# A two-layer block on one core: the first mixer's row shifts move from GpSimd's DMA queue to ACT's, with the gate job first and the parameter loads in three parts

## The reference

```
mod = silu(c) @ ada_w + ada_b                      # six rows of 1024: shifts, scales, gates
h = rms_norm(x, norm1_g) * (1 + sc1) + sh1
z = h @ w_in                                       # 2072 columns for fox, 1824 for rwkv
# fox (8 heads of 64)
k = a_k * shift_prev(k) + (1 - a_k) * k            # a_k = sigmoid of a gate column; v likewise
q, k = rms_norm(q), rms_norm(k)
cum = cumsum(log_sigmoid(f_logit + forget_b))      # over the tokens
o = softmax(causal(q k / 8 + cum_q - cum_k)) v
# rwkv (8 heads of 64)
zr = zr + mu * (shift_prev(zr) - zr)               # over all 1824 columns: r, k, v, low-rank parts
w, a, g = low-rank products of tanh / sigmoid parts of zr
o = wkv7_scan(r, w, k, v, -kk, kk * a)
x = x + g1 * (concat(fox, rwkv) @ w_out)
```

## Time and profile before

| | us |
|---|---|
| median of three timed runs (lowest, highest) | 1726.18 (1723.91, 1727.97) |
| the profiled execution | 1728.36 |
| its span in the profile | 1726.4 |
| TensorE busy, share of the span | 1420.5, 82% |
| DVE, ACT, POOL busy | 677.0, 392.9, 130.2 |

### The profile page before, as it was taken

How to read it: one execution, slowest core, us unless ns; L and a number is a source line. 1 busy time by engine, 2 the same in 40 slices (tenths; PEclk the granted TensorE clock), 3 DMA queues, 4 the chain that set the end, 5 groups by cost and what they waited for, 6 DMA issues and landing times.

```text
span 1726.4 us, 17781 instructions
## 1 busy us (share of the span) xinstructions
PE 1420.5 (82%) x6756; PEld 892.2 (52%) x6756; DVE 677.0 (39%) x1203; ACT 392.9 (23%) x620; POOL 130.2 (8%) x51
## 2 busy tenths in 40 slices
PE   5865845667897899999999999589968667599996
PEld 1432414666754444444444444366546436399974
DVE  2006227544446322222222222453365522457652
ACT  0101114132101121222222122234220111344442
POOL 0012224284000000000000000000000000000000
PEclk8887965787987899999999999689859987699998
DMA  9732101153127099999999997644411121145551
GB/s 326 215 122 74 47 17 72 57 186 126 49 90 309 36 402 422 412 420 409 416 421 420 415 413 302 229 146 146 75 48 50 49 98 49 49 149 171 170 172 72
DMA packets 105390, 338.76 MB, mean 196 GB/s; under 512 B 20465, under 2 KB 46484, under 8 KB 76537
## 3 DMA queue, kind: packets, MB, share of 16 engines
q1 hardware_dynamic: 84162, 319.08, 48.2%
q10 hardware_dynamic: 9528, 15.46, 3.3%
q0 software_dynamic: 11648, 3.50, 0.9%
HBM read 332.94 MB, written 1.05 MB: 193 GB/s over the span
## 4 chain that ended last, share of the span: by engine, by line
PE 68%; DVE 15%; DMA 5%; another core or an unknown queue 3%; ACT 3%; issue 2%; ACTq 2%; POOL 1%; DVEq 0%; SPq 0%; POOLq 0%
PE bank L1621 13%; PE bank L1637 7%; PE bank L1221 6%; PE bank L1240 6%; PE bank L1242 5%; PE bank L1241 5%; DMA z_prev<-z_rw 3%; PE bank L1584 2%; PE bank L1442 2%; DMA ring<-in_w_in 2%; PE bank L1585 2%; PE bank L1602 2%; PE bank L1604 2%; PE bank L1252 2%
## 5 line engine op out<-in xcount | busy, mean ns | idle before, releaser
L1221 PE MATMUL bank<-ring,xT 128*128 128x512 f32 (+3 forms) x480 | 203.0, 579 | 47.5 <-ACT z_rw L801 20.6
L1221 PEld LDWEIGHTS bank<-ring,xT 128*128 128x128 f32 x480 | 94.6, 213 | 146.3 <-issue 119.6
L1637 PE MATMUL bank<-dn,tmp 128*64 128x512 f32 x528 | 120.6, 598 | 0.0
L1240 PE MATMUL bank<-mod,w_high 128*128 128x256 f32 x352 | 101.6, 289 | 11.5 <-DVE xT L2948 5.3
L2574 DVE TENSOR_TENSOR xT<-bank,mod 128x512 fp32r<-128x512 f32 x66 | 45.7, 692 | 157.9 <-ACT mod L998 150.6
L1241 PE MATMUL bank<-xT,w_high 128*128 128x256 f32 x352 | 99.9, 284 | 0.0
L2567 DVE SCALAR_TENSOR_TENSOR tmp<-silu_c,rc,bank 128x256 f32<-128x256 f32 x33 | 22.6, 686 | 196.8 <-ACT silu_c L985 191.4
L1242 PE MATMUL bank<-mod,ring 128*128 128x256 f32 x352 | 99.5, 283 | 0.0
L2937 DVE TENSOR_TENSOR ring<-ring,w_high 128x1024 fp32r<-128x1024 f32 x66 | 77.6, 1220 | 26.2 <-ACT w_high L1163 24.6
L1252 PE MATMUL bank<-c_ident,xn 128*128 128x128 f32 x120 | 28.0, 412 | 63.7 <-DVEq L2637 25.4
L2015 POOL TENSOR_TENSOR ring<-ring 128x2048 f32<-128x2048 f32 x16 | 72.9, 4557 | 77.5 <-ACT ring L893 76.9
(11 more groups left out here) (581 smaller groups left out, 2563.1 us busy)
## 6 DMA issues: line engine op xcount, KB each, us to landing
dn<-in_exp_w_down SPq DMA_DIRECT2D x66, 1024.0 KB, 10.6
ring<-in_exp_w_gate SPq DMA_DIRECT2D x34, 1024.0 KB, 9.0
ring<-in_exp_w_up SPq DMA_DIRECT2D x34, 1024.0 KB, 10.8
gu_odd<-in_exp_w_gate SPq DMA_DIRECT2D x32, 1024.0 KB, 10.1
gu_odd<-in_exp_w_up SPq DMA_DIRECT2D x32, 1024.0 KB, 12.2
ring<-in_w_ffn_in SPq DMA_DIRECT2D x22, 1024.0 KB, 5.1
ring<-in_ada_w SPq DMA_DIRECT2D x16, 1024.0 KB, 4.9
ring<-in_w_in SPq DMA_DIRECT2D x7, 2048.0 KB, 27.8
```

The lines of the kernel that those rows point to most:

```text
L1221: mm = pe.matmul(bank[lin_bank(o)][:, 0:n], lhs(k, t), ring[:, j % RING, k * n:(k + 1) * n], start=(k == 0), stop=(k == kt - 1 and not bias))
L1240: pe.matmul(out, w[0], x[0], start=start, stop=False, skip_group_check=True)
L1637: mm = pe.matmul(bank[6 + h][CHUNKS[c], :], act_eT[:, 0, k, CHUNKS[c]], dn[:, 2 * parity + c, lo:lo + BANK], start=(k == 0), stop=(k == D_ ...
```

## The change

- The gate columns become the first input job; their copies, the gate sigmoid and the forget chain move to the head of ACT's list, and PE's small sum stands behind the key job.
- ACT issues the three fox gains and `mu` first, the constants and low-rank matrices after the key copies, and the seven rwkv rows and norm2_g after the value copies and the shift of keys and values.
- All five shifts are issued by ACT, each when the copies of its group are done; for KR and VR also after the lerp that used the same buffer two groups before. POOL keeps the row clears and the lerps.
- The receptance copies stand ahead of the two roots.
- Semaphores follow: `forget_loaded` counts four loads, `mu_loaded` is new, `par_loaded` counts the constants too, `zr_shifted` is one per buffer.

```diff
-        IN_JOBS = [(512, 512), (1024, 512), (2048, 24), (0, 512),
+        IN_JOBS = [(2048, 24), (512, 512), (1024, 512), (0, 512),
                    (FOX_COLS + 1536, 288), (FOX_COLS, 512), (FOX_COLS + 512, 512), (FOX_COLS + 1024, 512), (1536, 512)]
...
+            def shift_rows(dst, src, landed):
+
+                act.dma_start(dst[1:P, :, :], src[0:P - 1, :, :]).then_inc(landed, 16)
+                act.dma_start(dst[0:1, 1, :], src[P - 1:P, 0, :]).then_inc(landed, 16)
+
+            def shift_group(i, j):
+
+                lo, width = IN_JOBS[j]
+                act.wait_ge(lin_evac, after(j, 1))
+                if i >= 2:
+                    act.wait_ge(lerp_done, i - 1)
+                shift_rows(z_prev[:, i % 2, :, 0:width], z_rw[:, :, lo - FOX_COLS:lo - FOX_COLS + width],
+                           zr_shifted[i % 2])
...
+            for t in range(T):
+                in_copy(J_K, t)
             for name in CONST_1:
-                act.dma_start(cst[name][:, :], consts[name]).then_inc(const1_loaded, 16)
...
+                act.dma_start(cst[name][:, :], consts[name]).then_inc(par_loaded, 16)
...
+            for t in range(T):
+                in_copy(J_V, t)
+            act.wait_ge(lin_evac, after(J_V, 1))
+            shift_rows(kv_prev, z_fox[:, :, 512:1536], kv_shifted)
+            for i, name in enumerate(("rw_w0", "rw_a0", "rw_k_k", "rw_k_a", "rw_r_k", "rw_lnx_g", "rw_lnx_b")):
+                act.dma_start(rwp[:, i, :], bcast(A[name])).then_inc(par_loaded, 16)
             act.dma_start(gain[:, 1, :], bcast(A["norm2_g"])).then_inc(gain_loaded[1], 16)
...
+            for t in range(T):
+                in_copy(J_Q, t)
+            for i, j in enumerate((J_LORA, J_R)):
                 for t in range(T):
                     in_copy(j, t)
+                shift_group(i, j)
             rstd(fs[:, 6, 0:16], fs[:, 5, 0:16])
             rstd(fs[:, 8, 0:16], fs[:, 7, 0:16])
-            for t in range(T):
-                in_copy(J_R, t)
             act.wait_ge(lerp_done, 1)
...
             for t in range(T):
                 in_copy(J_KR, t)
+            shift_group(2, J_KR)
...
                     in_copy(J_VR, h - 1)
+                    if h == 2:
+                        shift_group(3, J_VR)
...
+            dense(J_FG, first_lhs)
+            dense(J_K, xTk)
             pe.wait_ge(logf_ready, 1)
...
-            for j in (J_LORA, J_R, J_KR):
+            for j in (J_V, J_Q, J_LORA, J_R, J_KR):
                 dense(j, xTk)
...
-                pool.dma_start(prev[1:P, :, :], z[0:P - 1, :, :]).then_inc(zr_shifted, 16)
-                pool.dma_start(prev[0:1, 1, :], z[P - 1:P, 0, :]).then_inc(zr_shifted, 16)
-                pool.wait_ge(zr_shifted, 32 * (i + 1))
+                pool.wait_ge(zr_shifted[i % 2], 32 * (i // 2 + 1))
```

More of the change, by code:

```diff
@@ L413, in build @@
         par_loaded = sem("par_loaded")
-        const1_loaded = sem("const1_loaded")
         ada_full = [sem(f"ada_full{i}") for i in range(ADA_RING)]
@@ L419, in build @@
         forget_loaded = sem("forget_loaded")
+        mu_loaded = sem("mu_loaded")
         ada_evac = sem("ada_evac")
@@ L433, in build @@
         sq_done = sem("sq_done")
-        pad_zero = sem("pad_zero")
         kv_shifted = sem("kv_shifted")
-        zr_shifted = sem("zr_shifted")
+        zr_shifted = [sem(f"zr_shifted{i}") for i in range(2)]
         lerp_done = sem("lerp_done")
@@ L552, in job @@
             jobs.append((kind, lo, n, kt, parts, bias is not None))
-        IN_JOBS = [(512, 512), (1024, 512), (2048, 24), (0, 512),
+        IN_JOBS = [(2048, 24), (512, 512), (1024, 512), (0, 512),
                    (FOX_COLS + 1536, 288), (FOX_COLS, 512), (FOX_COLS + 512, 512), (FOX_COLS + 1024, 512), (1536, 512)]
-        J_K, J_V, J_FG, J_Q, J_LORA, J_R, J_KR, J_VR, J_G = range(len(IN_JOBS))
+        J_FG, J_K, J_V, J_Q, J_LORA, J_R, J_KR, J_VR, J_G = range(len(IN_JOBS))
         for lo, n in IN_JOBS:
@@ L826, in _ @@
             for i, name in enumerate(("fox_qn_g", "fox_kn_g", "fox_on_g")):
-                act.dma_start(fxp[:, i, :], bcast(A[name])).then_inc(par_loaded, 16)
-            for name in CONST_1:
-                act.dma_start(cst[name][:, :], consts[name]).then_inc(const1_loaded, 16)
[L830 to L837, removed]
+                act.dma_start(fxp[:, i, :], bcast(A[name])).then_inc(forget_loaded, 16)
+            act.dma_start(mu[:, :], bcast(A["rw_mu"])).then_inc(mu_loaded, 16)
             def in_copy(j, t):
@@ L842, in in_copy @@
                 lin_copy(j, t, z_fox[:, t, lo:lo + n] if lo < FOX_COLS else z_rw[:, t, lo - FOX_COLS:lo - FOX_COLS + n])
-            for j in (J_K, J_V, J_FG):
-                for t in range(T):
-                    in_copy(j, t)
+            def shift_rows(dst, src, landed):
[9 more added lines that the diff above has]
+            for t in range(T):
+                in_copy(J_FG, t)
             act.wait_ge(lin_evac, after(J_FG, 1))
@@ L855, in _ @@
             act.activation(fs[:, 4, 0:16], fs[:, 3, 0:16], ACT.Ln, bias=1.0).then_inc(fox_ln, 1)
-            for j in (J_Q, J_LORA):
+            for t in range(T):
+                in_copy(J_K, t)
+            for name in CONST_1:
+                act.dma_start(cst[name][:, :], consts[name]).then_inc(par_loaded, 16)
+            act.dma_start(lora_up[0:DECAY_R, :], A["rw_decay_up"]).then_inc(par_loaded, 16)
+            act.dma_start(lora_up[DECAY_R:P, :], A["rw_iclr_up"]).then_inc(par_loaded, 16)
+            act.dma_start(gate_up[:, 0, :], A["rw_gate_up"][0:P, :]).then_inc(par_loaded, 16)
+            act.dma_start(gate_up[0:GATE_R - P, 1, :], A["rw_gate_up"][P:GATE_R, :]).then_inc(par_loaded, 16)
+            for t in range(T):
[4 more added lines that the diff above has]
+                act.dma_start(rwp[:, i, :], bcast(A[name])).then_inc(par_loaded, 16)
+            act.dma_start(gain[:, 1, :], bcast(A["norm2_g"])).then_inc(gain_loaded[1], 16)
+            for t in range(T):
+                in_copy(J_Q, t)
+            for i, j in enumerate((J_LORA, J_R)):
                 for t in range(T):
                     in_copy(j, t)
+                shift_group(i, j)
             rstd(fs[:, 6, 0:16], fs[:, 5, 0:16])
             rstd(fs[:, 8, 0:16], fs[:, 7, 0:16])
-            for t in range(T):
-                in_copy(J_R, t)
             act.wait_ge(lerp_done, 1)
@@ L1299, in first_lhs @@
                 return xTk(k, t)
-            for j in (J_K, J_V, J_FG, J_Q):
-                dense(j, xTk if j != J_K else first_lhs)
+            dense(J_FG, first_lhs)
+            dense(J_K, xTk)
             pe.wait_ge(logf_ready, 1)
@@ L1344, in low_rank_products @@
                 c = slice(t * P, (t + 1) * P)
-                pe.wait_ge(par_loaded, 16 * 15)
+                pe.wait_ge(par_loaded, 16 * (11 + len(CONST_1)))
                 pe.wait_ge(tp_evac, TP_LORA + 2)
@@ L1356, in decay_sums @@
             def decay_sums(t):
-                pe.wait_ge(const1_loaded, 16 * len(CONST_1))
+                pe.wait_ge(par_loaded, 16 * (11 + len(CONST_1)))
                 pe.wait_ge(logw_ready, t + 1)
@@ L1983, in link @@
                 pool.wait_ge(pool_chain, n[0])
[L1985 to L1990, removed]
+            pool.wait_ge(mu_loaded, 16)
             for i, j in enumerate((J_LORA, J_R, J_KR, J_VR)):
@@ L2093, in _ @@
                     .then_inc(h_ready, 1)
-            dve.memset(kv_prev[0:1, 0, :], 0.0).then_inc(pad_zero, 1)
-            dve.wait_ge(forget_loaded, 16)
+            link(dve.memset(kv_prev[0:1, 0, :], 0.0))
+            dve.wait_ge(forget_loaded, 16 * 4)
             dve.wait_ge(lin_evac, after(J_FG, 1))
@@ L2103, in _ @@
             dve.tensor_tensor(fs[:, 5, 0:16], fs[:, 1, 0:16], fs[:, 4, 0:16], ALU.subtract).then_inc(logf_ready, 1)
+            dve.wait_ge(sc_mm, SC_CUMF + 1)
+            link(dve.tensor_copy(fs[:, 1, 0:16], bank[6][:, 0:16]))
+            dve.sem_inc(sc_evac, 1)
             dve.wait_ge(fox_gates, 1)
@@ L2113, in _ @@
             dve.wait_ge(lin_evac, after(J_Q, 1))
-            dve.wait_ge(sc_mm, SC_CUMF + 1)
-            link(dve.tensor_copy(fs[:, 1, 0:16], bank[6][:, 0:16]))
-            dve.sem_inc(sc_evac, 1)
             for t in range(T):
@@ L2124, in _ @@
             dve.wait_ge(rstd_done, rstd_n[0])
-            dve.wait_ge(par_loaded, 16 * 15)
             for t in range(T):
@@ L2243, in decayed @@
                 dve.sem_inc(til_ready, 1)
-            dve.wait_ge(const1_loaded, 16 * len(CONST_1))
+            dve.wait_ge(par_loaded, 16 * (11 + len(CONST_1)))
             masked_scores(0)
```

## The result

| | before | after |
|---|---|---|
| median (lowest to highest), us | 1727.08 (1723.91 to 1730.28), 6 runs | 1712.4 (1710.9 to 1720.7), 6 runs |
| ratio, 95% interval | | 0.9927 (0.9900 to 0.9954) |
| the profiled execution, span | 1728.36, 1726.4 | 1711.08, 1709.2 |
| mean granted clock | 0.877 | 0.882 |

14.7 us faster in the medians, 17.3 between the two profiled executions. 23.3 were forecast. By the two traces 14.9 us arise in the first mixer: the copies into tilT begin at 279.32 (294.24 before). The rest of the program is 2.3 us shorter, which is less than the executions of one kernel differ.

What follows compares the result with a forecast made beforehand. The first mixer was taken to wait for SBUF-to-SBUF shift copies, each on one DMA engine. Key norms -16.4, last lerp -5.9 and gate job -1 gave -23.3 us: median 1726.2 to 1703, range 1672 to 1726.

Steps and rivals of the forecast that it cites:

- The rate: Shifts on ACT's queue: 127 rows still pass one DMA engine at 26 GB/s, 40.0 us for keys and values.
- the rival of 16 engines: Shifts on ACT's queue: spread over 16 engines, each lands in 3 to 4 us; 1646 us in all, chance 0.10.
- What ACT pays: ACT's list: each shift's issue holds ACT for half the shift, moving the first exponential to 188, +10.
- The 16.4 us at the key norms: First mixer, DVE: key norms start without stall at 215.8 for 232.2, -16.4 us.
- The last term: POOL's last lerp in the first mixer: ends before three DVE passes that it slowed begin, -5.9 us.
- Gate first: Start of the input jobs: DVE's wait for the norm1_g copy may shrink by 0 to 2.6 us, 1 taken.
- Receptance copies: ACT's list, roots behind these copies: DVE gets the roots at 163; the gain from the root ahead is lost to the queue.
- Parameters: ACT's 24 parameter issues, about 0.46 us each: only moved, hidden with over 30 us to spare, eight sharing the shifts' queue.
- The sum: Whole program: -16.4 at the key norms, -5.9 for the last lerp, -1 for the gate job, -23.3 us.
- Rival D: Shifts on ACT's queue: slower rows, 18 GB/s, engine's sum 165 us, keys landing at 242; 1743 us in all, chance 0.13.
- one engine's sum: Shifts, parameters and weight-load shares passing one DMA engine in the first mixer: 119 us, with 5 added 124.

Runs made afterwards that it cites:

- the cuts: Each 127-row copy cut: into 112 and 15 in the changed kernel (1651.93 us; POOL's queue 1652.59) and the kernel before (1655.57), into 126 and 1 in the changed (1650.61).
- the POOL experiment: The changed kernel with all five shifts issued by POOL again, everything else as changed: 1727.26 us, ratio 1.0008.

## Why the forecast held, and where it was off

| us | forecast | after |
|---|---|---|
| kv_prev landed | 128 | 127.6 |
| PE at the low-rank job | 112 | 122.7 |
| low-rank shift landed | 154 | 157.5 |
| receptance, key shift landed | 178, 200 | 184.7, 205.0 |
| roots | 163 | 173.1 |
| q_aug and k_aug ready | 172.7 | 180.3 |
| first exponential | 188 | 197.8 |
| key norms | 215.8 | 226.0 |
| fourth exponential | 222 | 236.3 |

- **The rate** (26 GB/s on one engine): right. kv_prev, the largest, landed within 0.5 us, the key lerp ended at 212.2 for 207.5. That the rival of 16 engines was a matter of the row count and not of the queue is shown by the cuts; its 1646 is near the 1650 to 1656 they took.
- **What ACT pays**, the mis-sized term. The mechanism was the forecast's, but for one point: the forecast put the hold at the long issue itself, and that one took 0.83 us; it is the issue behind it that is held. The size was 10 us short, all at the keys and values. ACT was to stand 20 us at the shift and until 112 at the parameters; it stood 36.87 us at the shift, 17 more, then 11.7 at the parameters, 7 less, and came to the query copies at 121.97. From 72 to 110 us 166 packets of some 4 KB (0.68 MB) passed on q10, 78 of them up to 90 us and 88 behind it, nearly all rows of kv_prev: some 90 of its 254 rows were left when the hold ended, where I had 134 left of them. Those 46 rows are 7 us at 26 GB/s. Another 8 are the sixteenth of the weight loads that passed the same engine meanwhile (3.28 MB on q1 from 72 to 110 us), which my 20 us for this hold had left out. A shift with nothing ahead of it shows the same size: at the value shift ACT is held 14.21 us, in which 155 rows pass, so some 100 are left. The query copies, the low-rank job, the roots, the first exponential and the key norms are then all some 10 us behind the forecast, one after another.
- **The 16.4 us at the key norms** so became 6.1 (232.16 to 226.03). The stall of 26.53 us is gone as forecast; DVE simply comes there 20 us later than it did.
- **The last term**, 5.9 us for the lerp beside DVE: right, 5.9 from the pass at 253.07 to tilT (26.25 us for 32.12).
- **Left out**: 2.9 us between the key norms and that pass (27.04 us for 29.96), a gain that made up by luck for part of what was missing. Before, PE had stood idle for 22.5 us ahead of the low-rank products and came back at half the clock; after, it had worked through. First before, then after:

```profile
232.00:246.00 14.00, 7.64 (x13) 2.73 (x13) 8.40 (x15) 0.99 (x4) 4.77 (x4) 0.50 0.11 11
```

```profile
226.00:240.00 14.00, 12.23 (x38) 5.49 (x38) 8.15 (x16) 3.70 (x8) 0.00 (x0) 1.00 0.07 27
```

A granted clock of 0.50 is the level of 1.2 GHz, 1.00 that of 2.4. A pair of products on gate_up took 2.07 us there and takes 1.12 here; two such pairs stand in a row ahead of DVE's gate copy, which is 1.9 us. The small products of the head behind them are 1.5 us shorter (2.75 for 4.28), and the input tile behind those takes 7.03 us for 9.47, 2.4 less; first before, then after:

```profile
247.99 9.47 PE L1221 MATMUL bank<-ring,xT 128*128 128x512 f32 x16
```

```profile
241.38 7.03 PE L1241 MATMUL bank<-ring,xT 128*128 128x512 f32 x16
```

That makes 5.9. Against it PE reaches the low-rank products 3.0 us later after the key norms than before (8.5 for 5.5), since it now has an input tile to do first: 2.9 are left.

- **Gate first**: forecast 1. The first h is 3.7 us earlier in this trace (33.67 for 37.38), 2.1 to 3.7 over all traces, since norm1_g is no longer waited for; what arrives in the stage is not shown to differ from nothing. **Receptance copies**: nothing, as forecast. **Parameters**: not run by themselves. The eight behind the shift held ACT for 11.7 us with the query copies behind them, which the forecast had in its 112. Together with the gate the three brought nothing on POOL's queue.
- **The sum**, from the spans: -6.1 - 2.9 - 5.9 and 2.3 behind the stage make -17.2, for -16.4 - 5.9 - 1.
- **Misread, without weight**: ACT issued 22 parameter loads in a row, not 24. q_aug and k_aug were ready at 161.55 (161.38 + 0.17), not 161.45. Rival D's sum of 165 ends at 240.5, not 242.
- My expectation for the POOL experiment was wrong by 30 us: I took the time of the shifts as given by one engine's sum, and overlooked that POOL's own list (lerp, then issue) keeps a ready shift from being queued, and that the low-rank one is complete only behind kv_prev.

## What to carry over

Look at the rate of a single copy before asking who issues it: 25 GB/s in a window where nothing else runs was the finding, and one cut of 127 rows into 112 and 15 was worth nearly five times the whole change (72 us for 14.7). Behind a long copy on one engine, ACT's queue held the next issue, not the copy's own; leave no issue directly behind it, and keep it off an engine whose list others wait for. A long new wait in a trace can be free (32.6 us for the roots): ask what stands behind it in the same list.

## What was not expected of the hardware

- On ACT's queue the issue of one 4 KB row took 36.87 us, that of the 127 rows before it 0.83.
- On POOL's queue the issue of 127 rows takes 3.8 us and that of 112 rows 0.86; on ACT's 0.83 and 0.76 (for the 15 rows 0.99).
- Of the eight parameter issues behind the shift seven took about 1.5 us each (L870 and L871, 1.30 to 1.64), where the same kind took 0.46 with the queue free.
- On POOL's queue two shifts under way move 0.25 MB in 6 us, 42 GB/s beside 0.05 MB of a load (two engines); on ACT's never more than 26 to 27 stands in any window with shifts alone. In spite of it the low-rank shift is complete on POOL's queue only when kv_prev is: 154.06 for 148.15.
- Between a shift and the rest of a weight load on one engine the split was 0.10 to 0.05 MB; so the load, too, is late by its last sixteenth. In the kernel with the shifts back on POOL, PE waits for such a load until 110.7, while from 106 to 112 us only 0.05 MB of it pass.
- The landing times that the issue rows give for POOL's long copies (8.3 to 11.5 us) are not those of the data: DVE waited for the 1016 KB until 135.29, 65 us after the issue at 69.83.
